# A sixteen-pair expert layer: how outputs get back to their tokens, where the row fetches stand, and which projection hosts the row stage

## The reference, cut to what matters

```python
x = layer_norm(DEEPNORM_ALPHA * x + g1x * yx, ln1_g[l], ln1_b[l])
ux = x * (1.0 + s2x) + sh2x
tok = ux.reshape(bn * t, d)                    # layer 0: and the context's tokens
y = hier_moe(tok, ...)
x = layer_norm(DEEPNORM_ALPHA * x + g2x * y, ln2_g[l], ln2_b[l])

def hier_moe(z, ...):                          # 32 experts, 2 for each token
    ...                                        # group, two experts of it, two weights comb
    def run(args):
        xb, e = args                           # a block of tokens, all of expert e
        h = jax.nn.silu(xb @ w_gate[e]) * (xb @ w_up[e])      # 1024 -> 512
        return h @ w_down[e]                                  # 512 -> 1024
    ys = lax.map(run, (xs, blk_exp)).reshape(p_rows, d)
    out = jnp.zeros((n + 1, d), z.dtype).at[row_tok].add(ys * row_w[:, None])
    return out[:n]
```

## Time and profile before

| | |
|---|---|
| median of three executions | 2556.48 us (2555.92 to 2559.42) |
| profiled execution | 2554.5 us, span 2552.7 us, mean granted clock 0.952 |
| TensorE products / weight loads | 2211.4 us (87%) / 1197.4 us (47%) |
| VectorE / ScalarE / GpSimd | 856.7 (34%) / 372.9 (15%) / 140.6 us (6%) |
| DMA | 697.43 MB, mean 273 GB/s |
| first hosting projection | 41.9 to 252 us |
| expert stage, layer 0 | 444 to 947 us |
| row stage, layer 0 | to 990 us |
| second hosting projection | 990.8 to 1137 us |
| expert stage, layer 1 | 1272 to 1774 us |
| row stage, layer 1 | to 1808 us |

### The profile page before, as it was taken

One profiled execution on the slowest core, in us unless ns is written; L12 is line 12 of the kernel. 1 busy time (PEld: TensorE's weight loads), 2 busy tenths in 40 slices (PEclk: granted clock), 3 DMA queues, 4 the chain that ended last, 5 costly groups with the idle time before them and its releaser, 6 DMA issues. The chain is left out here.

```text
span 2552.7 us, 35100 instructions
## 1 busy us (share of the span) xinstructions
PE 2211.4 (87%) x14023; PEld 1197.4 (47%) x14024; DVE 856.7 (34%) x1532; ACT 372.9 (15%) x627; POOL 140.6 (6%) x206
## 2 busy tenths in 40 slices
PE   6999977998888865996797888886899999989999
PEld 2444744443333323444432333223566777766776
DVE  1564667410000006868622100001453233492001
ACT  1000413111111111015111111111151000110000
POOL 1001010000000012000000000001110010000000
PEclk8999988999999986999799999998899999999999
DMA  9767421999999966780499999997323886534442
GB/s 351 294 252 297 151 69 76 393 423 422 423 422 423 422 270 211 281 315 6 152 416 421 423 423 423 423 423 305 140 96 142 307 301 235 170 104 149 149 150 81
DMA packets 176956, 697.43 MB, mean 273 GB/s; under 512 B 14149, under 2 KB 72517, under 8 KB 114416
## 3 DMA queue, kind: packets, MB, share of 16 engines
q1 hardware_dynamic: 159456, 624.86, 62.8%
q0 software_dynamic: 11968, 51.00, 5.6%
q10 hardware_dynamic: 5456, 20.53, 2.2%
HBM read 673.09 MB, written 22.20 MB: 272 GB/s over the span
## 5 line engine op out<-in xcount | busy, mean ns | idle before, releaser
L1626 PE MATMUL bank<-ring,arena 128*32 128x512 f32 (+1 forms) x3072 | 356.9, 613 | 79.6 <-DMA ring<-moe_w_up 52.8
L510 PE MATMUL bank<-ring,actT 128*128 128x512 f32 x768 | 339.3, 602 | 4.2 <-DMA ring<-ab_w_in 3.0
L2737 PE MATMUL bank<-actT,ring 128*128 128x256 f32 x1344 | 293.3, 379 | 0.0
L2737 PEld LDWEIGHTS bank<-actT,ring 128*128 128x128 f32 x1344 | 255.2, 190 | 42.3 <-issue 8.6
L1626 PEld LDWEIGHTS bank<-ring,arena 128*32 128x32 f32 x3072 | 100.3, 112 | 330.8 <-issue 329.0
L1643 PE MATMUL bank<-arena 128*32 128x512 f32 (+1 forms) x2048 | 226.6, 594 | 25.7 <-ACT arena L1717 24.8
L510 PEld LDWEIGHTS bank<-ring,actT 128*128 128x128 f32 x768 | 146.9, 193 | 195.6 <-issue 191.3
L1758 DVE TENSOR_TENSOR arena<-arena,bank 128x512 f32<-128x512 f32 x32 | 22.0, 688 | 612.9 <-ACT arena L1715 612.9
L587 DVE SCALAR_TENSOR_TENSOR arena<-ring,cols,arena 128x2048 f32<-128x2048 f32 x70 | 162.7, 2349 | 78.2 <-DMA ring<-ada_w 76.9
L2094 PEld LDWEIGHTS bank<-arena 128*128 128x128 bf16 x2448 | 139.9, 99 | 32.3 <-issue 26.8
L2749 PE MATMUL bank<-ring,arena 128*128 128x512 f32 x352 | 154.6, 593 | 0.0
(11 more groups left out here) (459 smaller groups left out, 2054.7 us busy)
## 6 DMA issues: line engine op xcount, KB each, us to landing
ring<-moe_w_gate SPq DMA_DIRECT2D x128, 1024.0 KB, 24.5
arena<-moe_w_down SPq DMA_DIRECT2D x128, 1024.0 KB, 21.7
ring<-ada_w SPq DMA_DIRECT2D x72, 1024.0 KB, 7.5
ring<-ffn_w SPq DMA_DIRECT2D x66, 1024.0 KB, 5.3
ring<-moe_w_up SPq DMA_DIRECT2D x64, 1024.0 KB, 23.7
actT<-moe_w_up SPq DMA_DIRECT2D x64, 1024.0 KB, 24.6
arena<-ada_w POOLq DMA_DIRECT2D x24, 1024.0 KB, 9.6
made_scratch<-arena ACTq DMA_DIRECT2D x32, 512.0 KB, 7.8
```

The source lines that it names most:

```text
L510: mm = nc.tensor.matmul(self.bank[g % 6][:, :], lhsT(m, k), halves[k // 4][:, k % 4, :], start=(k == 0), stop=(k == KT - 1))
L1626: mm = nc.tensor.matmul(bank[j // 2][Q * q:Q * q + Q, :], A(XS + P * kt + Q * q, Q), weights(j, own, q, k * DE, DE), start=(kt == 0), stop ...
L2737: mm = nc.tensor.matmul(bank[2 - 2 * (j % 2) + which][:, f * SEQ:(f + 1) * SEQ], w[:, k, f * P:(f + 1) * P], self.actT[:, k * T:k * T + SE ...
```

## The change

1. **Layer 1's expert stage doesn't store to `made`.** After each pair VectorE has prepared, for the pair's 128 rows, a matrix SHARE of each token's weight (new `shares`: the comparison of the row numbers with the pair's places, times the weights), TensorE transposes it (two products into bank 3), ScalarE copies it to TURNED, and once YS is there TensorE adds TURNED times YS into four banks that stay open over all pairs (`combine`: two tiles by two halves). The open banks are 4 to 7, so down goes to banks 1 and 2; up therefore waits for YS to have left bank 1, and the gather is cut in two halves, one ahead of the transposes and one behind down. The tables move ahead of pair 0, the overflow places and the context's preparation each one or two pairs earlier.
2. **The last pair stands apart, behind the overflow pairs**, in both layers, and gathers nothing. In layer 0 it isn't stored: VectorE builds the weights of the last pair's rows, TensorE transposes them within the down products, and the next stage multiplies them with YS in SBUF.
3. **Fetches beside the last pair** (layer 0): GpSimd waits for the store of the pair before and for the last pair's down weights, then fetches all eight tiles of rows; tokens whose row is the last pair's get a harmless row and weight 0 (`rows_to_fetch`). VectorE adds the first tile in the expert stage. SyncE issues the next two weight loads as soon as the last pair has used gate and up.
4. **The row stage of layer 0 goes into the projection** (`rows_before_c`): TensorE begins with the last pair's products, VectorE adds and modulates tile by tile and now also scales the first fetched row; groups are ordered so that those of token tile 0 of the first three chunks come first (they need fetched tiles 0 and 1); the transposes of tiles 2 and 3 stand ahead of group 3. All three first chunks are loaded at the start; modulation units begin at group 4.
5. **Layer 1's row stage** begins with the last pair's combination and adds the banks to x.
6. **The first projection's round (0,1)** is weighed by VectorE instead of TensorE (`AB_ON_PE`). The scratch clears two more blocks.

```diff
+C_ORDER = [(0, 0), (1, 0), (2, 0), (0, 1), (1, 1), (2, 1), (2, 2), (2, 3)] + [(ci, m) for ci in (3, 4, 5) for m in range(4)]
+C_FIRST, C_LATE = 3, 4
+FRONT_TURNS, FRONT_USES = {0: (0, 1), 3: (2, 3)}, {0: 1, 3: 3}
-AB_ON_PE, C_ON_PE = (0,), ()
+AB_ON_PE, C_ON_PE = (), ()
+SUMMED = ((6, 7), (4, 5))
...
+                if front is not None:
+                    front["mix"](pe)
...
+                    if front is not None:
+                        for t in FRONT_TURNS.get(g, ()):
+                            front["turn"](pe, t)
+                        if g in FRONT_USES:
+                            front["taken"](pe, FRONT_USES[g])
...
+        down_bank = (4, 5) if layer == 0 else (1, 2)
...
+                        if layer and j == 2:
+                            pe.wait_ge(sc["made"], p + (first + 1))
...
-                    pe.wait_ge(sc["picked"], p + (first + 2))
-                    gather_pair()
+                    if not last:
+                        pe.wait_ge(sc["picked"], p + (first + 2))
+                        gather(0)
+                        if layer == 0:
+                            gather(1)
...
+                    if layer:
+                        pe.wait_ge(sc["weighed"], p + (first + 2))
+                        for t in range(nt):
+                            mm = nc.tensor.transpose(bank[3][:, t * P:(t + 1) * P], A(SHARE + t * P, P), self.ident)
+                        mm.then_inc(sc["w_turned"], 1)
...
+                    if layer and not last:
+                        pe.wait_ge(sc["w_taken"], p + (first + 1))
+                        gather(1)
+                        pe.wait_ge(sc["made"], p + (first + 2))
+                        for t in range(nt):
+                            mm = self.combine(t, False)
+                        mm.then_inc(sc["mixed"], 1)
...
-                with pe.Fori(0, PAIRS) as p:
-                    pair(p, 0, main_arrived)
+                with pe.Fori(0, LAST) as p:
+                    pair(p, 0, bass.ds(p, 1), lambda m: main_arrived(p, m))
                 pe.wait_ge(sc["tables"], 1)
                 there = blocks(pe)
                 with pe.Fori(0, NOV) as q:
                     with pe.If(there > 2 * q):
-                        pair(q, PAIRS, over_arrived)
+                        pair(q, LAST, bass.ds(q + PAIRS, 1), lambda m: over_arrived(q, m))
+                pair(extra_pairs(pe), LAST, slice(LAST, LAST + 1), lambda m: main_arrived(LAST, m), last=True)
...
+                more = extra_pairs(sp)
+                load_pair(more, LAST - 1, slice(LAST, LAST + 1))
+                sp.wait_ge(sc["used"], more * 6 + (6 * LAST + 4))
+                self.feed(sp, 2)
...
+                    pool.wait_ge(sc["rows"], 1)
+                    pool.wait_ge(self.spare_in[0][3], 16 * PAIRS)
+                    self.fetch(pool, nt, IDX, 0)
+                    pool.wait_ge(self.spare_in[0][5], 16 * PAIRS)
+                    for t in range(1, nt):
+                        self.fetch(pool, nt, IDX, t)
...
+    def combine(self, t, stop, shares=None, to=None):
+        lhsT = self.A(TURNED + t * P if shares is None else shares + t * P, P)
+        for c in range(2):
+            mm = self.nc.tensor.matmul(self.bank[SUMMED[t][c] if to is None else to + c][:, :], lhsT, self.A(YS + 512 * c, 512),
+                                       start=to is not None, stop=stop, skip_group_check=True)
...
+            add_last(0)
+            for t in range(1, 4):
+                self.add_fetched(dve, link, t)
+                modulate(t - 1)
+                add_last(t)
+            modulate(3)
```

535 lines of the change are left out of this document (334 added, 201 removed).

## The result

The changed kernel takes 2521.26 us (median of four executions, 2516.83 to 2523.07) against 2556.25 for the kernel before beside it: ratio 0.9856, 95% interval 0.9842 to 0.9871. Run again beside the last experiment it took 2519.08 against 2554.17 (0.985, 0.9831 to 0.9868). The forecast was 2497, its own range 2486 to 2506, and for 8 in 10 2484 to 2516: the direction is right, but the time lies outside both ranges, and 35 us came where 59 were forecast.

The account below looks back on a forecast made before the run. Bounds: DMA in expert stages, TensorE in the two hosting projections, the serial stretch after each expert stage. From 2554.5: -4 (Part 5), -21.4 (Part 4 with its share of Part 3), -34.5 (Parts 1, 2), +2: 2497; range 2486 to 2506, 8-in-10 2484 to 2516.

Parts of the forecast that it names:

- Part 1: Layer 1's expert stage: without stores a pair takes 29.8 us instead of 31.02, DMA still setting the pace; -18.6 us.
- E1: The forecast's name for layer 1's expert stage, the second, with two token tiles.
- (a): Layer 1's expert stage becomes bound by TensorE, 30.8 us a pair, 16 us lost: 2513; chance 0.17.
- (d): Layer 1's expert stage: granted clock falls under the load, pairs stretch, slower than before, 2595 at 0.8; chance 0.02.
- Part 2: Layer 1's last pair and row stage: query latent's projection starts at 1774, 34.5 us earlier, Part 1's 18.6 included.
- Part 3: Skipped overflow bodies ahead of the last pairs: 0.53 us a pass; 1.2 stays in layer 0, none in layer 1.
- E0: The forecast's name for layer 0's expert stage, the first, with four token tiles.
- Rival (b): Skipped overflow bodies cost instruction fetches, 1.7 us a pass, 13.6 and 6.8 in the two stages: +15, 2512; chance 0.10.
- (c): The projections don't gain: VectorE late for round 0, first projection as before; +10, 2507; chance 0.10.
- Part 4: Layer 0's expert-stage end and second projection: first group 25.8 us earlier, 4.4 back at group 3, hosted work follows; net -21.4.
- Part 5: First projection: round (0,1) moves from TensorE to VectorE; bounds 0 and -5.8 us, -4 taken.

Follow-up runs that it names:

- the last experiment: Changed kernel with one outer test around each overflow loop on all engines and a second adaLN bias buffer in the second projection, run once more: 2515.93 us.
- before_small_store: Kernel before the change with the 16 stores of layer 1's expert stage cut to 4 of 1024 columns: 2535.1 us.
- no_overflow: Changed kernel with the loops over overflow pairs dropped on every engine: 2518.6 us (2505.2 to 2522.2).
- all_none2: Changed kernel without overflow loops, with second bias buffer and TensorE's round sums one group later, its take wait kept only for TensorE's own rounds: 2508.6 us.
- after: The changed kernel itself, all parts of the change against the kernel before: 2521.26 us, ratio 0.9856.

## Why the prediction was right in direction and wrong in size

**Part 1 (E1 without stores) was right.** Period 29.82 where DMA sets it (forecast 29.8), 28.92 where TensorE does (28.75), loads at 422 GB/s, and before_small_store gave 17.9 of the 18.6 us. Rivals (a) and (d) are out: the granted clock from 1400 to 1700 is 1.00.

**Part 2 was right in its chain.** From the end of the last down product to the query latent's projection it is 26.7 us (1752.9 to 1779.60), forecast 28.5. It only began late. Parts 1 and 2 together, E1 without the loops, are 494.4 us for a forecast 495.0.

**Part 3 was the step that failed.** It took 1.2 us in E0 and 0 in E1 for the skipped bodies, from ScalarE's 0.53 a pass. Dropping the loops was worth 5.7 us in E0 and 9.6 in E1, 15 us for a forecast 1.2. The passes themselves were sized about right: 0.62 to 0.81 measured. What was missing is the fixed 6.0 us that comes with TensorE's long body, with a fetch of instructions in it. Taking the price from "four more passes take 2.14 us" drops any fixed part before it is looked at; ScalarE's walk had one of 1.6 us, and no row was TensorE's. Then I let slack absorb what was left. E1 had no such slack: the hole stood there in full. With the lower clock behind the hole (12.44 instead of 10.51) E1 lost 9 us. E0 lost 10, of a hole of 12.46 and 1.5 on the same block (11.98), and there 4.3 of the 10 are not the loops' but part 4's.

**Rival (b) named the cause and nearly the size**: +15 from 13.6 and 6.8 us of holes; measured 12.46 and 8.45. Its mechanism was a fetch for each pass, which is not so. I gave it 0.10, although the only row about it came from another engine; its 2512 was inside my range, and with the second projection's 8 us the kernel fell outside. Rivals (b) and (c) added, +15 and +10, give 2522, which is near the measured 2521; that is partly luck, as (c) supposed no gain in the first projection and there was a part of it.

**Part 4's row stage was right, its hosted work not.** From E0's products to the first group it is 27.5 us (946.61 to 974.10), forecast 27.2; without the loops (no_overflow, all_none2) it is 29.2 and 29.1, with products of 8.8 instead of 7.1 us behind the longer wait. The end of E0 ahead of it, set by GpSimd's fetches there, was 2.3 us late. The hole at group 3 was 2.8 in all (997.74 to 1000.55) instead of 4.4. But for the hosted units I took 4 us from the freed slot to the first landing. Group 3 frees its slots at 1004.1 in after, the load is issued at 1007.72 and the weights are there at 1018.98: 15 us. Round 0 was ready 3.6 us after TensorE asked for it, and the last unit at 1120.9, 102 us after the first, not 89, since VectorE waits for loads in between. I also looked at takes and stores nowhere: the chain from round 1's take to the stage's end is 20.7 us long and became what ends last. Wait 3.64, low clock 1.72, wait 0.52 and 2.88 more at the end than before (4.72 for 1.84) make 8.8, less 1.6 at group 3: 7.2 of the 8 us. This is VectorE being late for round 0, as in rival (c), and it happened together with (b).

**Part 5** was half of its size. In the one trace of after it gave 4.7 us at its stage's end, near the forecast 4, and 3.8 of them were gone at E0; but that trace is one of fifteen, and on average it gave 2 us at both places. The agreement at the stage's end was luck. What parts these traces isn't shown; in the attention stage behind it the granted clock differs between them, first after, then before:

```profile
250.00:276.00 26.00, 25.31 (x95) 15.81 (x94) 13.78 (x16) 13.39 (x17) 1.15 (x3) 0.80 0.85 315
```

```profile
250.00:276.00 26.00, 23.29 (x100) 13.20 (x99) 14.17 (x16) 11.96 (x18) 1.65 (x3) 1.00 0.74 266
```

**Still open.** all_none2 has neither loops nor the shared bias buffer and still takes 2508.6 us. Its profile has the first group at 969.97, 9 us later than the forecast's 961.0: E0 began 4.3 late, the products, held by the fetches, come 2.8 later still (940.86), and the row stage is 1.9 longer. The next stage stands at 1128.44, 15.5 late: 6.5 more, with a wait of 3.4 for VectorE's last sum and 7.37 instead of 1.84 at the end. How much more a better order of the hosted rounds could give was not tried, nor was hiding the fetch of instructions, by taking TensorE's jump where it waits anyway.

## What to carry to other kernels

A branch over a long body can cost its engine several us even if the body never runs. Price it on that engine, with that body, fit a fixed part beside the price of a pass, and look at the profile's instruction queue. Where a skipped body moves ahead of work that sets the end, put one test around the whole loop. Count a stretch from its own start before you compare two traces: here the same code began up to 9 us apart, and that made some forecasts look better than they were. When a stage gets shorter, follow its latency chains (take, store, reload of one buffer) to the end: they don't shrink with it, and waits ahead of them may cost nothing. Of two rivals with different causes, ask what both together give before setting the range.

## What the runs showed of the hardware

TensorE's one jump over the pair's body left a hole of 5.5 to 6.8 us in every one of eight profiles (6.57 to 6.83 in E0, of which 0.45 are there without a loop too; 5.48 to 5.70 in E1), with DMA at 422 GB/s. A packet of instructions of 16 KB takes 1.0 to 1.1 us of a DMA engine in it; the second of the two starts when TensorE works again. Behind such a hole TensorE's granted clock is lower for a while (0.59 from 910 to 920, 0.90 in the next 10 us), and 96 records that take 10.51 us took 12.0 to 13.4. Behind E1's 2.48 us hole they took 10.51. The same code reached E0 anywhere from 447.0 to 456.1 us and took 738.5 to 747.6 us from the query latent's projection to the end, and executions of one kernel lay up to 18 us apart, so an effect under some 5 us needs the stretch's own rows, from more than one profile, and not the medians of five runs.
